# Recurrence levels as 64 by 64 products on two column halves, with an earlier and less even schedule

## The reference

```python
b = jnp.cumsum(fb, axis=2)
diff = b[:, :, :, None, :] - b[:, :, None, :, :]
decay = jnp.exp(jnp.where(lower_tri, diff, -jnp.inf))
scores = jnp.einsum("bhtk,bhsk,bhtsk->bhts", qb, kb, decay)
o_intra = jnp.einsum("bhts,bhsv->bhtv", scores, vb)
```

## Time and profile before

| | |
|---|---|
| median of 3 runs | 2034.56 us (2034.24 to 2035.13) |
| the profiled execution | 2034.4 us, its span 2032.6 us (1.8 us lie outside the span) |
| mean granted TensorE clock | 0.996 |
| PE busy | 1991.4 us, 98% of the span |
| DVE busy | 1267.7 us, 62% |
| ACT busy | 1065.8 us, 52% |
| DMA | 352.69 MB, mean 174 GB/s |
| the four rounds of the recurrence | from 483.4 us (first turn) to about 944 us |

### The profile page before, as it was taken

One profiled execution on the slowest core, in us unless ns is written; L12 is line 12 of the kernel. 1 busy time (PEld: TensorE's weight loads), 2 busy tenths in 40 slices (PEclk: granted clock), 3 DMA queues, 4 the chain that ended last, 5 costly groups with the idle time before them and its releaser, 6 DMA issues.

```text
span 2032.6 us, 25932 instructions
## 1 busy us (share of the span) xinstructions
PE 1991.4 (98%) x9504; PEld 1659.7 (82%) x9504; DVE 1267.7 (62%) x1727; ACT 1065.8 (52%) x1356; POOL 201.3 (10%) x91
## 2 busy tenths in 40 slices
PE   7999999999999999999999998999999999999999
PEld 6888878888888888888887886888888888888887
DVE  5699956545968777785667674544454454444443
ACT  6444456546667585864547673544444444433332
POOL 0899740000000000000000000000000000000000
PEclk9999999999999999999999998999999999999999
DMA  8655545565545454545564333656655565656654
GB/s 296 194 186 184 171 132 195 168 207 166 156 154 154 143 160 134 156 134 176 166 207 137 113 109 110 197 189 195 191 189 189 173 197 191 193 192 191 194 193 159
DMA packets 182841, 352.69 MB, mean 174 GB/s; under 512 B 11616, under 2 KB 12000, under 8 KB 182752
## 3 DMA queue, kind: packets, MB, share of 16 engines
q1 hardware_dynamic: 181184, 350.27, 54.3%
q10 hardware_dynamic: 1568, 1.23, 0.2%
HBM read 349.36 MB, written 2.10 MB: 173 GB/s over the span
## 4 chain that ended last, share of the span: by engine, by line
PE 80%; DVE 11%; ACT 5%; issue 2%; DVEq 1%; DMA 0%; ACTq 0%; SPq 0%
PE acc L377 24%; PE acc L379 24%; PE acc L378 24%; DVE T L1030 7%; PE T L478 3%; PE T L359 2%; ACT w_hi L637 1%; DVE w_lo L975 1%; DVEq L967 1%; ACT sm L904 0%; PE T L488 0%; PE T L487 0%; PE T L558 0%; PE T L442 0%; ACT E L812 0%
## 5 line engine op out<-in xcount | busy, mean ns | idle before, releaser
L975 DVE TENSOR_TENSOR w_lo<-raw,w_hi 128x1024 fp32r<-128x1024 f32 x576 | 699.2, 1223 | 607.2 <-ACT w_hi L637 599.9
L637 ACT ACTIVATE w_hi<-raw 128x1024 fp32r<-128x1024 f32 x656 | 683.5, 1058 | 537.2 <-PE acc L379 518.7
L377 PE MATMUL acc<-w_hi,h_hi 128*128 128x512 f32 x1888 | 746.8, 396 | 15.0 <-DVE h_lo L987 13.0
L379 PE MATMUL acc<-w_hi,h_lo 128*128 128x512 f32 x1888 | 737.2, 390 | 0.0
L378 PE MATMUL acc<-w_lo,h_hi 128*128 128x512 f32 x1888 | 736.5, 390 | 0.0
L377 PEld LDWEIGHTS acc<-w_hi,h_hi 128*128 128x128 f32 x1888 | 355.7, 188 | 88.8 <-DVE h_lo L987 13.0
L379 PEld LDWEIGHTS acc<-w_hi,h_lo 128*128 128x128 f32 x1888 | 355.1, 188 | 74.8
L378 PEld LDWEIGHTS acc<-w_lo,h_hi 128*128 128x128 f32 x1888 | 355.8, 188 | 70.9
L346 POOL TENSOR_TENSOR w_lo<-raw,w_hi 128x1024 fp32r<-128x1024 f32 x80 | 189.8, 2408 | 89.9 <-ACT w_hi L637 89.6
L1030 DVE SCALAR_TENSOR_TENSOR T<-vpad,feat,T 128x256 f32<-128x256 f32 x464 | 182.4, 479 | 0.0
L377 PE MATMUL acc<-w_hi,y_hi 128*128 128x512 f32 x384 | 154.5, 402 | 7.4 <-DVE w_lo L975 5.2
(11 more groups left out here) (200 smaller groups left out, 1364.9 us busy)
## 6 DMA issues: line engine op xcount, KB each, us to landing
raw<-in_hgrn_w_in_dram SPq DMA_DIRECT2D x160, 512.0 KB, 3.6
raw<-in_conv_w_in_dram SPq DMA_DIRECT2D x96, 512.0 KB, 3.9
raw<-in_ffn_w_gate_dram SPq DMA_DIRECT2D x88, 512.0 KB, 4.4
raw<-in_ffn_w_up_dram SPq DMA_DIRECT2D x88, 512.0 KB, 4.2
raw<-in_ffn_w_down_dram SPq DMA_DIRECT2D x88, 512.0 KB, 4.7
raw<-in_attn_w_qkv_dram SPq DMA_DIRECT2D x40, 512.0 KB, 3.9
raw<-in_conv_w_out_dram SPq DMA_DIRECT2D x32, 512.0 KB, 4.2
raw<-in_hgrn_w_out_dram SPq DMA_DIRECT2D x32, 512.0 KB, 4.9
```

Of the source, the lines that this page charges most:

```text
L377: nc.tensor.matmul(o, hi[:, kt, a], w_hi[:, slot, kk, :], start=kt == 0, stop=False)
L379: last = nc.tensor.matmul(o, lo[:, kt, a], w_hi[:, slot, kk, :], start=False, stop=kt == p.chunks * CK - 1)
L637: A(w_hi[:, slot, :, :], raw[:, slot, :, :], ACT.Copy).then_inc(hi_ready, 1)
L975: TT(w_lo[:, slot, :, :], raw[:, slot, :, :], rounded(w_hi[:, slot, :, :]), ALU.subtract).then_inc(split_ready, 1)
```

## The change

1. The products of level 0 and of levels 2 to 8 become 16 of 128 features by 64 keys by 64 queries (4 heads, 4 runs of 64 positions; level 2 couples neighbouring runs). Those of odd runs write PSUM partitions 64 to 127, those of even runs 0 to 63. Level 1 stays 8 products of 128 by 128. The score blocks that are not written any more were masked or overwritten anyway.
2. The steps in front of the levels move to earlier ticks, often two into one.
3. Level s hangs at the ticks of a list, two apart up to level 5, then 3, 2 and 3 apart. What hung relative to a level stays so.

```diff
+WEIGH_AT = [0, 10, 12, 14, 16, 18, 21, 23, 26]
...
# PE, level(j, s)
+                c = P if s == 1 else P // 2
                 for h in range(HPG):
-                    for b in range(2):
-                        o = T[:, h // 2, (h % 2) * S + b * P:(h % 2) * S + b * P + P]
-                        sl = slice(b * P, (b + 1) * P)
-                        tl = slice((1 - b) * P, (2 - b) * P) if s == 1 else sl
-                        g, q = (e[:, 1, h, sl], qT[:, h, tl]) if s == 0 else (e[:, 0, h, sl], e[:, 1, h, tl])
-                        last = nc.tensor.matmul(o, g, q, start=True, stop=True)
+                    for i in range(S // c):
+                        o = i ^ 1 if s in (1, 2) else i
+                        keys, queries = slice(i * c, (i + 1) * c), slice(o * c, (o + 1) * c)
+                        r, at = i * c % P, (h % 2) * S + (i if s == 1 else o) * c
+                        g, q = (e[:, 1, h, keys], qT[:, h, queries]) if s == 0 else (e[:, 0, h, keys], e[:, 1, h, queries])
+                        last = nc.tensor.matmul(T[r:r + c, h // 2, at:at + c], g, q, start=True, stop=True)
# PE, process(j)
-                at = Hooks().put(0, lambda: turn(j, 0, qtok)).put(1, lambda: turn(j, 1, aftok)).put(2, lambda: turn(j, 2, abtok))
-                at.put(7, lambda: level(j, 0))
+                at = Hooks().put(0, lambda: turn(j, 0, qtok)).put(0, lambda: turn(j, 1, aftok)).put(1, lambda: turn(j, 2, abtok))
+                at.put(5, lambda: level(j, 0))
-                    at.put(10 + 2 * s, lambda s=s: level(j, s))
+                    at.put(WEIGH_AT[s] - 1, lambda s=s: level(j, s))
# ACT, process(j)
-                at = Hooks().put(3, lambda: q_copy(j)).put(4, lambda: gates(j, 0)).put(5, lambda: gates(j, 1))
+                at = Hooks().put(3, lambda: q_copy(j)).put(3, lambda: gates(j, 0)).put(4, lambda: gates(j, 1))
-                    at.put(6 + d, lambda d=d: ln_f(j, d)).put(8 + d, lambda d=d: ln_k(j, d))
-                at.put(10, lambda: take(j, 0))
+                    at.put(5 + d, lambda d=d: ln_f(j, d)).put(6 + d, lambda d=d: ln_k(j, d))
+                at.put(8, lambda: take(j, 0))
-                    at.put(11 + 2 * s, lambda s=s: exp(j, s))
+                    at.put(WEIGH_AT[s], lambda s=s: exp(j, s))
-                        at.put(13 + 2 * s, lambda s=s: take(j, s))
+                        at.put(WEIGH_AT[s] + 2, lambda s=s: take(j, s))
# DVE, process(j)
-                at = Hooks().put(2, lambda: bounds_of(j)).put(6, lambda: diagonal(j)).put(8, lambda: scan_f(j)).put(9, lambda: scan_b(j))
-                at.put(10, lambda: keys(j, 0)).put(11, lambda: keys(j, 1)).put(12, lambda: diffs(j, 1))
+                at = Hooks().put(2, lambda: bounds_of(j)).put(5, lambda: diagonal(j)).put(6, lambda: scan_f(j)).put(7, lambda: scan_b(j))
+                at.put(8, lambda: keys(j, 0)).put(8, lambda: keys(j, 1)).put(9, lambda: diffs(j, 1))
-                        at.put(11 + 2 * s, lambda s=s: take(j, s - 1))
-                    at.put(11 + 2 * s, lambda s=s: weigh(j, s))
+                        at.put(WEIGH_AT[s - 1] + 2, lambda s=s: take(j, s - 1))
+                    at.put(WEIGH_AT[s], lambda s=s: weigh(j, s))
-                        at.put(12 + 2 * s, lambda s=s: diffs(j, s + 1))
-                at.put(29, lambda: take(j, 8))
+                        at.put(WEIGH_AT[s] + 1, lambda s=s: diffs(j, s + 1))
+                at.put(28, lambda: take(j, 8))
```

## The result

| | before | after |
|---|---|---|
| median of 8 runs each | 2034.19 us | 2040.78 us (2039.83 to 2041.36) |
| ratio | | 1.0033, interval [1.0024, 1.0042] |
| profiled execution, span | 2034.4, 2032.6 us | 2041.0, 2039.2 us |

A forecast was written before the change was run, and what follows sets the result against it. PE, busy 98% of the span, was taken as the bound. Three rounds' 6.0 us, the fourth's +3.1 and the clock's +2.0 gave +11 on the profiled 2034.4, so 2045.5 us; 8-in-10 range 2036 to 2061.

The forecast's parts named there:

- The level: On PE, each of 32 levels with products on two column halves: 1.38 us instead of 1.80, 13.4 us less in all.
- halves that take turns: Rival at the levels: column halves don't run together, a level grows to 2.26 us; +29, 2063 us; chance 0.10.
- issue: Rival at the levels: instruction issue paces the 32 matmuls, a level takes 3.1 us; about +50, 2084 us; chance 0.03.
- The front: Last turn to level 1: ACT and DVE need 28.2 us, PE 24.0, so PE waits 4.2 us more each round.
- The case of the covered front: Rival at weigh(1): ACT and DVE arrive within PE's 24.0 us, only shorter levels count; -8.4, 2026 us; chance 0.10.
- The levels behind: After level 1: level 2 comes 0.8 us late, and waits of 0.8 us in all stay at levels 5 and 7.
- The rounds: Shorter levels against added waits, by round: +2.0 us in each of the first three, +3.1 in the fourth, together +9.1.
- The clock: Granted clock falling to 0.50 behind level 1's idle time: two falls in four rounds, +2.0 us; bounds none and 6.6.

The follow-up runs named there:

- the grouped order: e3 with each level's 8 products of even runs issued before the 8 of odd runs, instead of alternating: 2042.18 us, ratio 1.0042.
- e2: The change without its new level products, so the new ticks alone with the products of before: 2052.66 us, ratio 1.0090 against the kernel before.
- e3: The changed kernel with all levels one to two ticks later and the last take at 29, the front unchanged: 2022.31 us, ratio 0.9939.
- e5: e3 with the steps in front reordered, among them both ln_f before ln_k and both scans at tick 6: 2012.79 us, ratio 0.9893.
- e6: The changed kernel with ln_k of the forward direction on 16 of 256 columns: 2037.46 us, ratio 1.0018 against the kernel before.
- e9: The changed kernel, levels at its own ticks, with only the front in e5's order and take(0) left at 8: 2032.80 us, ratio 0.9987.
- e8: e3 with all levels two ticks apart and the last take at 27: 2030.36 us, ratio 0.9982 against the kernel before.
- e4: The changed kernel with 8 unused matmuls of 512 columns in front of level 1's wait in each round: 2041.70 us, ratio 1.0037.

## Why the prediction was right

**The level.** Forecast 1.38 us, measured 1.31: 16 pairs 0.058 apart, which is 0.93, and about 0.4 for getting into the column halves and out of them, as I took it from the earlier trace rows. The rule of the Trainium skill (TensorE: Matmul & The Clock Gate, "Wait — 56ns, not 53.3ns?") of about 62 ns for each matmul where the sequencer decodes in software is not what this trace shows: the level's row with 32 matmuls spans 1.15 us, where the rule would give 1.98, an estimate. The rivals of halves that take turns and of issue are out; the grouped order is what the first of them looks like, and its level of 2.06 us stays under the 2.26 that I gave it.

**The front.** Forecast: 28.2 us of ScalarE and VectorE against 24.0 of PE, a wait of 4.2, in pieces before the chunks of ticks 8 and 9 and before level 1. Measured in the second round: 4.2 us by starts, in those three places. The chain came out link by link, not by luck of the sum:

```profile
600.29 1.04 PE L360 MATMUL T<-ident,abtok 128*128 128x128 f32 x8
...
602.06 1.03 ACT L791 ACTIVATE E<-T 128x1024 f32<-128x1024 f32 x1
...
613.14 1.04 ACT L639 ACTIVATE w_hi<-raw 128x1024 fp32r<-128x1024 f32 x1
...
614.22 1.23 DVE L977 TENSOR_TENSOR w_lo<-raw,w_hi 128x1024 fp32r<-128x1024 f32 x1 [1.32 <-ACT w_hi L639]
```

From the last turn to its sigmoids 1.8 us (forecast 1.8), from there to the end of the rounding of tick 7 12.1 (12.15), from `w_lo` to level 1 at 628.49 14.3 (14.25): 28.2 us. The other rounds have 28.7, 28.2 and 28.0. e2 shows it without the new products, e3 takes it away with one chunk, e5, e6 and e9 by shortening the chain. The case of the covered front would have needed the chain to be shorter than its rows; it was not.

**The levels behind.** Forecast: 0.8 us at level 2, and 0.8 at levels 5 and 7 together. Measured in round 1 by starts: 0.75 at level 2, 0.5 and 0.35 at levels 5 and 7. In the second and third round, with their falls of the clock, the waits at levels 2 and 5 are gone. e8 shows VectorE's period.

**The rounds.** Forecast +2.0 each and +3.1 in the last, together 9.1. Measured +1.5, +1.45, +1.7 and +1.9, together 6.6. For the first three the shorter level explains it: 8 x 0.07 = 0.56 us less. It gives half of the 1.2 us that the last round is off. The other half is in the waits: I let them grow by 6.5 us, and they grew by 5.9 (1.94 and the 3.92 that its eight shorter levels save), the cost of a fall of the clock included. Which of its waits I had too long isn't shown.

**The clock.** This term failed: "I count two falls in four rounds, +2.0". There were three falls. In rounds 2 and 3 they cost next to nothing, shown by e4, which takes them away and gains 0.0 and 0.2 us, and by the change's own first round, which had none and was no shorter. What the third one cost, in the last round, isn't shown: in e4 the fall moves one level on there instead of going away. I let level 2's wait absorb half of a fall and forgot level 5's. Without this term the sum is 2043.5; with it 2045.5 was 4.7 us above the measured 2040.8, and inside the stated range.

So the direction and the mechanism were right. The size, 11 us forecast and 6.6 measured, was off by these terms, all on one side.

## What to carry to other kernels

When engines run side by side on one list of ticks, price a moved step by the chain that it belongs to: here 28.2 us of two engines against 24.0 of the third, both summed from rows, foretold the wait of 4.2 us. A shorter bottleneck pays only where the other engines have room: the same 15.7 us of TensorE work were worth 5, 11 or 16 us, as the schedule let them. Ticks that are late enough, and an order that (with other moves) puts VectorE's scans beneath ScalarE's logarithms, gave what drawing steps together could not.

## What the runs showed of the hardware

- Fp32 products of 128 by 64 by 64 on the two column halves overlap fully when they alternate (pairs 0.058 us apart, 0.029 us for each matmul with its load) and hardly when the 8 products of one half (16 matmuls and their 16 loads) stand before the other's: 0.058 us each, but for three pairs at the changeover. In attention the other half stood 8 instructions, loads included, behind and did overlap. Where between 8 and 32 it ends wasn't tried.
- Getting PE into and out of divided columns costs about 0.4 us together: of the 1.31 us of a level 16 pairs of 0.058 are 0.93, and 0.38 is left. The rows on divided rows gave the same.
- Falls of the granted clock to 0.50 followed idle times of 2.6 us in brackets, not each time: three of four in the change and in the kernel with the ticks alone. They also followed 2.0 and 2.1 us (e9, e4). What a fall costs depends on the waits behind it that can take it up: 0.0 and 0.2 us at level 1 of rounds 2 and 3, 1.5 us at level 2 of the last round in e4.
- A logarithm on 16 columns takes 0.38 us against 0.59 on 256: thinning the instruction to a sixteenth saved about a third of its time.
